# Query input of the PEER layer: which engine writes the high and the low parts

## The reference

```python
x = layer_norm(DN_ALPHA * x + g1 * mix, ln1_g[l], ln1_b[l])
h = layer_norm(x) * (1.0 + sc2) + sh2
ffn = peer(h, w_pq[l], sub_key_1[l], sub_key_2[l], u_table[l], v_table[l])

def peer(h, w_pq, sub_key_1, sub_key_2, u_table, v_table):
    q = jnp.dot(h, w_pq).reshape(B, S, PEER_HEADS, 2, PEER_KEY_DIM // 2)
    ...
```

## Time and profile before

| | us |
|---|---|
| median of the runs (3 runs) | 3156.36 |
| lowest and highest | 3153.74, 3160.82 |
| the profiled execution | 3157.6 |
| its span | 3156.0 |
| busy: PE, DVE, ACT, POOL | 3087.9, 2254.4, 1438.4, 711.6 |
| the stage of the change | 1624.8 to 1639.6 of the span |

### The profile page before, as it was taken

How to read it: one execution, slowest core, us unless ns; L and a number is a source line. 1 busy time by engine, 2 the same in 40 slices (tenths; PEclk the granted TensorE clock), 3 DMA queues, 4 the chain that set the end, 5 groups by cost and what they waited for, 6 DMA issues and landing times.

```text
span 3156.0 us, 43109 instructions
## 1 busy us (share of the span) xinstructions
PE 3087.9 (98%) x16124; PEld 2643.2 (84%) x16124; DVE 2254.4 (71%) x2683; ACT 1438.4 (46%) x1469; POOL 711.6 (23%) x513
## 2 busy tenths in 40 slices
PE   8999899999999988999989999999999999999998
PEld 6888788888888877888779888888888888888887
DVE  7766888888888878556688888766665555555556
ACT  5556544444444455446554443444444343434343
POOL 1100000000000000000002888888881101110110
PEclk9999999999999999999989999999999999999999
DMA  8444677777789865784435777888876766676763
GB/s 281 174 174 178 236 279 279 276 280 276 276 299 338 300 253 190 254 329 149 161 133 166 241 221 210 263 257 257 258 241 216 256 241 250 242 257 242 250 243 136
DMA packets 195361, 754.25 MB, mean 239 GB/s; under 512 B 53827, under 2 KB 53859, under 8 KB 124851
## 3 DMA queue, kind: packets, MB, share of 16 engines
q1 hardware_dynamic: 129988, 664.86, 58.4%
q0 software_dynamic: 55904, 70.92, 8.3%
q10 hardware_dynamic: 9360, 17.04, 1.5%
HBM read 714.82 MB, written 37.93 MB: 239 GB/s over the span
## 4 chain that ended last, share of the span: by engine, by line
PE 91%; DVE 4%; DMA 2%; ACT 1%; issue 1%; DVEq 0%; SPq 0%; ACTq 0%
PE bank L456 26%; PE bank L444 16%; PE bank L446 16%; PE bank L445 16%; PE bank L461 14%; DMA ring<-in_first 1%; DMA ring<-in_down 1%; PE bank L579 1%; DVE raw_lo L2168 0%; PE bank L926 0%; DVE misc L2332 0%; PE bank L450 0%; ACT ffn_hi L1533 0%; PE bank L567 0%; DVE raw_lo L2460 0%
## 5 line engine op out<-in xcount | busy, mean ns | idle before, releaser
L456 PE MATMUL bank<-h_both,ffn_hi 128*128 128x512 f32 x3440 | 820.6, 391 | 0.2 <-ACT ffn_hi L1719 0.2
L2915 DVE TENSOR_TENSOR part_lo<-ring,ffn_hi 128x2048 fp32r<-128x2048 f32 x254 | 582.3, 2293 | 324.2 <-ACT ffn_hi L2025 321.1
L2025 ACT ACTIVATE ffn_hi<-ring 128x2048 fp32r<-128x2048 f32 x250 | 479.2, 1917 | 611.9 <-PE bank L461 395.9
L456 PEld LDWEIGHTS bank<-h_both,ffn_hi 128*128 128x128 f32 x3440 | 633.1, 188 | 124.2 <-ACT ffn_hi L1719 0.6
L3273 POOL DMA_INDIRECT weight_dram<-misc x256 | 557.7, 2178 | 88.1 <-issue 75.7
L444 PE MATMUL bank<-ffn_hi,coef_hi 128*128 128x512 f32 x1008 | 392.1, 389 | 0.0
L445 PE MATMUL bank<-part_lo,coef_hi 128*128 128x512 f32 x1008 | 392.1, 389 | 0.0
L446 PE MATMUL bank<-ffn_hi,coef_lo 128*128 128x512 f32 x1008 | 392.1, 389 | 0.0
L2168 DVE TENSOR_TENSOR raw_lo<-ring,ffn_hi 128x2048 fp32r<-128x2048 f32 (+1 forms) x131 | 297.7, 2276 | 113.4 <-ACT ffn_hi L1533 112.4
L1533 ACT ACTIVATE ffn_hi<-ring 128x2048 fp32r<-128x2048 f32 x133 | 254.5, 1915 | 264.8 <-DMA ring<-in_first 99.8
L1719 ACT ACTIVATE ffn_hi<-ring 128x2048 fp32r<-128x2048 f32 x87 | 166.6, 1917 | 263.5 <-DMA ring<-in_gateup 261.4
(11 more groups left out here) (476 smaller groups left out, 4910.4 us busy)
## 6 DMA issues: line engine op xcount, KB each, us to landing
ring<-in_u_table SPq DMA_DIRECT2D x128, 1024.0 KB
ring<-in_v_table SPq DMA_DIRECT2D x128, 1024.0 KB
misc<-in_w_ada SPq DMA_DIRECT2D x192, 512.0 KB
ring<-in_gateup SPq DMA_DIRECT2D x88, 1024.0 KB
ring<-in_first SPq DMA_DIRECT2D x56, 1024.0 KB
ring<-in_down SPq DMA_DIRECT2D x44, 1024.0 KB
ring<-in_stream SPq DMA_DIRECT2D x40, 1024.0 KB
ring<-in_wo_pq SPq DMA_DIRECT2D x32, 1024.0 KB
```

Of the source, the lines that this page charges most:

```text
L456: nc.tensor.matmul(out[:, 0:2 * S], hi[:, k * P:(k + 1) * P], x_pair(k), start=k == 0, stop=False)
L2025: a.activation(part_hi[j % PARTS], raw[j % RAW], ACT.Copy).then_inc(sem("hi_ready"), 1)
L2915: v.tensor_tensor(part_lo[j % PARTS], raw[j % RAW], part_hi[j % PARTS].bitcast(F32), ALU.subtract).then_inc(sem("lo_ready"), 1)
```

## The change

For all sixteen groups of this input (not for n5), the work is divided into three steps on three engines: ScalarE writes the high part from the bank, with scale and shift; VectorE writes bank times scale, less the high part, into `pT[:, k % 2]`; GpSimd adds the shift and writes the low part. VectorE waits for low part k - 2 before it writes `pT` again. GpSimd's sixteen instructions stand behind its iotas, ahead of its waits for the experts.

```diff
+        def shifted_hi(a, k):
+
+            a.wait_ge(sem("x_turned"), TURN_AT["h2"] + k + 1)
+            a.activation(h2_hi[:, k, :], bank[4 + k % 4][:, 0:S], ACT.Identity, scale=modc[:, 0, k:k + 1],
+                         bias=modc[:, 1, k:k + 1]).then_inc(sem("x_hi_out"), 1)
+
+        def scaled_rest(v, k):
+
+            v.wait_ge(sem("x_hi_out"), TURN_AT["h2"] + k + 1)
+            if k >= 2:
+                v.wait_ge(sem("x_lo_out"), TURN_AT["h2"] + k - 1)
+            v.scalar_tensor_tensor(out=pT[:, k % 2, :], in0=bank[4 + k % 4][:, 0:S], scalar=modc[:, 0, k:k + 1],
+                                   in1=h2_hi[:, k, :].bitcast(F32), op0=ALU.mult, op1=ALU.subtract).then_inc(
+                sem("h2_rest"), 1)
+
+        def shifted_lo(g_, k):
+
+            g_.wait_ge(sem("h2_rest"), k + 1)
+            g_.tensor_scalar(h2_lo[:, k, :], pT[:, k % 2, :], modc[:, 1, k:k + 1], None, ALU.add).then_inc(
+                sem("x_lo_out"), 1)
...
             for k in range(KD):
-                mod_hi(a, steps, "h2", k, h2_hi)
+                shifted_hi(a, k)
...
             for k in range(KD):
-                mod_lo(v, steps, "h2", k, h2_hi, h2_lo)
+                scaled_rest(v, k)
...
                 sem("iota_done"), 1)
 
+            g_.wait_ge(sem("modc_ready"), 2)
+            for k in range(KD):
+                shifted_lo(g_, k)
+
```

## The result

The changed kernel takes 3164.59 us (median of 13 runs, 3161.48 to 3168.59), the kernel before 3156.36 (13 runs, 3153.74 to 3160.82): a ratio of 1.0026 with a 95% interval of 1.0019 to 1.0034, 8.2 us slower. The forecast was 3158.7 with a range of 3152.0 to 3164.0, and "slower" had 0.08.

The account below looks back on a forecast made before the run. TensorE's row of matmuls was taken to bound the kernel, the stage counting through when low part 15 stands. Terms -0.9 + 2.1 + 1.1 = +2.3 us on the median 3156.4 gave 3158.7 us, range 3152.0 to 3164.0.

Parts of the forecast that it names:

- the rings: Buffer reuse in the query input stage from k = 4: pT ring 0.62 us a group, bank ring 0.60.
- rival B: GpSimd's shift becomes the bound; slower from about 1.05 us a group, 3169 at 1.5 us; chance 0.07.
- The prediction's own sign: Wrong in kind if the shift's mean is over 0.8 us or TensorE's idle time moves to another stage.
- The tail: Stage's end: shift 15 waits for VectorE's next lower part, starting 2.28 us after rest 15, not 0.2; +2.1 us.
- ScalarE and VectorE: Sixteen instructions each: ScalarE 551 ns, 8.8 us for 12.3; VectorE 483 ns, 7.7 for 11.1; ScalarE stops being slow.
- GpSimd's step: Each of sixteen 128x256 tensor_scalar shifts takes 0.45 us, bounds 0.19 to 0.74.
- Term one: Faster pace of the groups brings low part 15 earlier: -0.5 to -1.2 us, taken -0.9.
- Term two: The last shift waits for one whole VectorE lower part behind rest 15: +2.1 us.
- Term three: TensorE idles 2.2 to 2.4 us before the last group and its clock may halve: 0 to +3.0 us, taken +1.1.
- C: Shifts 14 and 15 are both held up by lower parts: +4.5 instead of +2.1, up to 3163.4 us; chance 0.05.
- A: The last shift isn't held up, so the gain of -0.5 to -1.2 us survives: 3155.5 us; chance 0.22.
- The sign to watch: In GpSimd's trace: fifteen shifts of 0.4 to 0.5 us and a last of 2.3 to 2.7 us.

Follow-up runs that it names:

- e2: The changed kernel with VectorE waiting for the last low part before it takes any of the next tiles' lower parts; 3158.2 us.
- e8: The changed kernel with a GpSimd copy in place of the shift, and VectorE waiting for the last low part before the next lower parts; 3155.4 us.
- e6: The changed kernel with 32 additional matmuls on TensorE ahead of the last group's wait, to fill its idle time; 3162.7 us.
- e3: The changed kernel with VectorE taking one tile's lower part, then waiting for the last low part before the other two; 3161.7 us.
- e7: The changed kernel with GpSimd copying pT into the low part, the shift left out; 3158.1 us.
- e4: The changed kernel with GpSimd adding the constant 0.0 in place of the shift column; 3161.5 us.
- e1: The kernel before with 24 extra GpSimd instructions on scratch space, tensor_scalar forms and copies, in GpSimd's empty stretch; 3154.5 us in one run.
- e5: The changed kernel with GpSimd adding the shift for even k, VectorE for odd k, and VectorE's next lower parts waiting; 3159.0 us.

## Why the prediction was wrong

The step that failed is the price of GpSimd's shift: taken at 0.45 us with an upper end of 0.74, it measured 0.91. With it went the mechanism that the forecast had for the pace, which was to come from the rings and TensorE's slot at 0.58 to 0.68 us a group; it came from GpSimd working without a pause, at 0.90, which is rival B's mechanism. The prediction's own sign says so: it called itself wrong in kind if the shift's mean was over 0.8 us, and the mean is 1.16. The tail was right in kind (the last shift loses to the next lower part) and wrong in its count, two hold-ups for one.

- *ScalarE and VectorE*: right, 0.56 and 0.48 us; ScalarE stopped being the slow one. A slip that no term uses: "4 x 0.12 = 0.35 us" is three products of 0.12.
- *GpSimd's step*, the term that failed. "Sum 0.42 to 0.46 us; I take 0.45", with an upper end of 0.74. It is 0.91, outside the bounds. I took the per-element rate of an affine_select and the fixed part of a copy and an iota for a tensor_scalar; the fixed part was right (0.21 us), the rate is 2.5 ns where I had 1.06, and doubling it for the upper end was not enough.
- *Term one*: taken -0.9 us, measured +2.2 (e2, 16.65 against 14.48). With a step of 0.40 us it is -1.6 (e8): for the price that was assumed, the argument about the rings holds; its input was wrong.
- *Term two*: taken +2.1, measured +3.8 (20.49 against e2's 16.65). "One waits for the other's whole instruction" held, with turns taken, as rows 6 and 7 had shown. What I missed is that a shift with its scalar in SBUF can lose two turns. The term had a single hold-up without a row for this form; the profile before had no instruction of that kind on GpSimd.
- *Term three*: taken +1.1, measured +1.7 by the window at 0.50 and +1.3 by e6. The idle time was 4.2 us and not 2.2 to 2.4, because of the second hold-up. With one hold-up the idle time is 1.9 to 2.1 us, and the clock stayed at 1.00 in two runs (e3, e7) and fell in one (e4), so that taking a part of the loss was fair.
- *The sum*: +2.2 + 3.8 + 1.7 = +7.7 against the +2.3 forecast.
- *The rivals*: B had the right place. At 0.91 us its formula gives 1627.5 + 15 x 0.91 + 2.1 = 1643.3, 4.1 us over the 1639.2 of before; I let it decide for slower from 1.05 us on, since it counted one hold-up and no clock. With two hold-ups (3.8) and the clock (1.7) the same formula passes +6.3 us from 0.83 us on. C saw two lower parts ahead of low part 15, but by way of shifts 14 and 15 losing one turn each; shift 14 wasn't touched. A fell with the changed kernel's own trace: the last shift, at 4.81 us, didn't get in first.
- *The sign to watch* that the prediction named, a last shift of 2.3 to 2.7 us, is what e3, e4 and e7 show; the changed kernel's 4.81 is one more turn. ScalarE's first tile behind the stage (L1533, now L1554), which was to start about 1 us earlier, started 13.9 us after the first turn in both kernels (1638.67 and 1638.13).

## What to carry to other kernels

Price an instruction by a row of the same operation on the same engine. Where there is none, another operation's rate is a weak bound: here tensor_scalar cost 2.3 times the affine_select's rate per element (2.5 against 1.06 ns), and twice was not enough. Look at what stands behind the last step in the other engine's queue: one VectorE instruction with two inputs in SBUF held up the waiting GpSimd instruction by 1.8 to 2.0 us (e3, e4, e7), and two of them held up the one with a scalar column by 3.9 (the changed kernel). So count the operands that the waiting instruction takes from SBUF, its scalar column among them. A wait that holds the long instruction back cost nothing else in e2, where its result is due later: one line gave back 5.3 us.

## What the runs showed of the hardware

- GpSimd, 128 partitions x 256 float32: tensor_scalar 0.85 us with a constant and 0.92 with a column, copy 0.40 (e1); VectorE does the same addition in 0.35 (e5).
- A GpSimd instruction with its scalar in SBUF was held up by two successive VectorE instructions (4.81 us), the same one with a constant by one (2.71 us), with the same three in its queue (changed kernel, e4).
- VectorE instructions with one input in PSUM and one in SBUF didn't hold up GpSimd's copies: 0.39 to 0.40 us each in e8.
- The length of the idle time alone doesn't decide on the clock. After 1.94 us it stayed at 1.00 (e7). After 2.05 us of idle time the clock stayed at 1.00 in e3 and was at 0.57 over 4 us in e4; these are e3's rows and then e4's:

```profile
1640.82 0.39 PE L444 MATMUL bank<-h_both,ffn_hi 128*128 128x256 f32 x1 [2.05 <-POOL h_both L747]
1640.80:1644.80 4.00, 3.98 (x33) 1.00 0.52 172
...
1643.41 0.42 PE L444 MATMUL bank<-h_both,ffn_hi 128*128 128x256 f32 x1 [2.05 <-POOL h_both L747]
1643.40:1647.40 4.00, 3.99 (x20) 0.57 0.55 168
```

What made the difference between these two stays open.
